# Forget values computed tile by tile, tokens stationary, in the first stage of a hybrid streaming encoder step

## The chip, the cores and the metric

The kernel runs on one core of a Trainium2 chip. The metric is device time in microseconds (us) of one execution; lower is better. The engines are TensorE (PE; its weight loads are a row of their own, PEld), VectorE (DVE), ScalarE (ACT), GpSimd (POOL) and SyncE (SP), which here only issues DMAs. Each engine works through its own instructions in order and waits at semaphores for the others.

## What is computed

One layer of a hybrid encoder, for 1024 tokens of a prompt and 8 x 16 tokens of running streams, 1152 tokens in all, with a model width of 1024:

```python
h = rms_norm(x, ln1)
proj = h @ w_in                       # columns: q 512, k 512, v 512, f 8, xr 512, yg 512
q, k, v, f, xr, yg = jnp.split(proj, SPLITS, axis=-1)
logf = jax.nn.log_sigmoid((f + b_f).astype(jnp.float32))   # one value a token and head
attn = fox_prompt(q, k, v, logf)      # attention with the cumulative sum of logf in its logits
...                                   # conv + RG-LRU on xr, gelu(yg), mixed @ w_out
x = x + jnp.square(jax.nn.relu(h2 @ w_up)) @ w_down
```

The change is about `f`: the product of h (1152 x 1024) with eight columns of `w_in`, the forget values before their log sigmoid.

## The kernel before, in words

All wide products are split: an operand is held as a rounded high part and a remainder (`h_hi`, `h_lo`; `wf_hi`, `wf_lo`; both of type fp32r), and `split_product` issues three matmuls for each of the 8 slices of the contraction (`KC` = 8): high x high, high x low and low x high, on lines 1383, 1384 and 1385, so 24 for one result. Each matmul has its own weight load of its stationary operand (the profile counts 7539 of either); two neighbouring matmuls that share one load it twice. Rows of the profile name the moving operand first and the stationary one second, `psum<-wp_hi,h_hi`.

**First stage.** For each of 9 tiles of 128 tokens (`NT` = 9): SP loads `x_in` into one of three slots, once `turn` of the tile three before has ended (line 405); ACT takes the sum of squares (line 696, one record for the activation and one for reading the accumulator); DVE makes the mean (955), POOL the root (606), DVE normalizes in place (`x_norm`, 959); PE transposes the tile in eight 128x128 pieces into two of four PSUM banks (`turn`, 1399); ACT casts the result to `h_hi` (`turn_hi`, 688) and DVE subtracts to get `h_lo` (`turn_lo`, 966). ACT and DVE do the casts of tile t-2 after the squares or the mean of tile t. `turn(t)` also waits for `h_lo` of tile t-2, whose banks it reuses. After tile 3, PE transposes the small parameter rows (1408). DVE copies them out ahead of `turn_lo(3)` (977).

After the nine tiles ACT and DVE split the forget weights `wf_raw` (704, 985) and then the weights of the first head pair (708, 989). PE computes the forget values: the eight weight columns stationary, 384 tokens moving, three groups (`G` = 3) of 24 matmuls into banks 5 to 7. ACT copies the 8 x 384 results to `f_rows` (715), and PE turns them in nine transposes into 128 tokens x 72 values in bank 4 (1421). DVE adds the bias and starts the log sigmoid (1003 to 1018); PE waits for `l_abs`, which line 1007 signals, because bank 4 is needed next.

**Pair stage.** `pair_pe(0)` projects tile after tile: `project(t)` is 24 matmuls of 384 columns with `h_hi` or `h_lo` of the tile stationary. After `project(1)` PE waits for the normed queries and keys of tile 0 (`turn_qk(0)`, 1456), which need a root from POOL (662). POOL does these roots only after it has built all constants (600 to 651), and it starts on most constants after the root of tile 8. `turn_forgets` follows `project(2)`. Then come the attention of four head pairs, the recurrent part, the output projection and the MLP, in program order throughout. No scheduler reorders anything: the order on each engine is the order written.

Of the kernel before, what the change touches and what calls it, by code (L numbers as in the profile page):

```python
# [7 lines left out]
F32 = mybir.dt.float32  # L8
F32R = mybir.dt.float32r
BF16 = mybir.dt.bfloat16  # L10
ALU = mybir.AluOpType
# [3 lines left out]
P = 128  # L15
# [5 lines left out]
H = 8  # L21
# [6 lines left out]
T_ALL = SEQ + DEC_B * DEC_T  # L28
NT = T_ALL // P
KC = D // P  # L30
G = 3
GN = T_ALL // G
# [27 lines left out]
def streaming_step(nc, x_prompt, x_sample, cache_k, cache_v, cache_logf, state_h, state_conv, ln1, w_in, b_f,  # L60
# [6 lines left out]
    def sem(name):  # L67
        return ctx.enter_context(nc.semaphore(name))

    def sb(scope, name, shape, dt=F32):  # L70
        return scope.enter_context(nc.sbuf_tensor(name, shape, dt))

    h_hi = sb(ctx, "h_hi", [P, KC, T_ALL], F32R)
    h_lo = sb(ctx, "h_lo", [P, KC, T_ALL], F32R)
# [7 lines left out]
    over = ExitStack()  # L82
# [6 lines left out]
    cc = sb(over, "cc", [64, KEYS])  # L89
    c_mid = sb(over, "c_mid", [64, KEYS], BF16)  # L90
    over_pad = sb(over, "over_pad", [P, 64])
    f_rows = sb(over, "f_rows", [H, T_ALL])
    over.close()
    under.close()
    mix = sb(ctx, "mix", [P, KC, T_ALL])
# [1 line left out]
    ident = sb(ctx, "ident", [P, P])  # L97
# [46 lines left out]
    wf_raw = sb(cross, "wf_raw", [P, KC, H])  # L144
    wf_hi = sb(cross, "wf_hi", [P, KC, H], F32R)
    wf_lo = sb(cross, "wf_lo", [P, KC, H], F32R)
# [60 lines left out]
    psum = ctx.enter_context(nc.psum_tensor("psum", [P, 8, 512], F32))  # L207
# [8 lines left out]
    wf_in = sem("wf_in")  # L216
# [8 lines left out]
    h_lo_ready = sem("h_lo_ready")  # L225
    rows_turned = sem("rows_turned")
    wf_split = sem("wf_split")
    f_done = sem("f_done")
    f_copied = sem("f_copied")
    f_turned = sem("f_turned")  # L230
    wf_ready = sem("wf_ready")
    params_copied = sem("params_copied")
    l_abs = sem("l_abs")
# [77 lines left out]
    def two_banks(b):  # L311
        return psum[:, b:b + 2, :].rearrange("p a n -> p (a n)")
# [29 lines left out]
    def step_queries(s):  # L342

        _, qc, kt = attention_step(s)
        return max(kt * P, qc * SPAN), (qc + 1) * SPAN
# [21 lines left out]
    with nc.allow_non_contiguous_dma(reason="narrow columns of small arrays"), nc.Block() as block:  # L367
# [313 lines left out]
        def _(act):  # L681
# [9 lines left out]
            for t in range(NT):  # L691
                act.wait_ge(x_landed[t % 3], 16 * (t // 3 + 1))
                if t >= 1:
                    act.wait_ge(x_squared, t)

                nc.scalar.activation(two_banks(6), x_in[:, t % 3, :], ACT.Square,
                                     accum_out=x_ss[:, t:t + 1]).then_inc(x_squared, 1)
                if t >= 2:
                    turn_hi(t - 2)
            turn_hi(NT - 2)  # L700
            turn_hi(NT - 1)

            act.wait_ge(wf_in, 16)
            nc.scalar.copy(wf_hi[:], wf_raw[:]).then_inc(wf_split, 1)

            def pair_hi(p, j):
                act.wait_ge(raw_in[j], 32 * p + 32)
# [2 lines left out]

            for j in range(4):
                pair_hi(0, j)
            for g in range(G):
                act.wait_ge(f_done, g + 1)
                nc.scalar.copy(f_rows[:, g * GN:(g + 1) * GN], psum[0:H, 5 + g, 0:GN]).then_inc(f_copied, 1)
            act.wait_ge(l_abs, 1)
            nc.scalar.activation(l_e[:], l_e[:], ACT.Exp, scale=-1.0).then_inc(l_exp, 1)

# [228 lines left out]
        def _(dve):  # L947
# [23 lines left out]
            for t in range(NT):  # L971
                x_mean_of(t)
                if t == 5:
                    dve.wait_ge(small_in, 16 * SMALL)
                    nc.vector.tensor_scalar(qgain[:], qgain[:], DH ** -0.5, None, ALU.mult)
                    dve.wait_ge(rows_turned, 1)
                    nc.vector.tensor_copy(param[:, :, 0:ROWS], psum[:, 4, 0:LC * ROWS].rearrange(
                        "p (c r) -> p c r", c=LC)).then_inc(params_copied, 1)
                if t >= 2:
                    turn_lo(t - 2)  # L980
                x_norm(t)
            turn_lo(NT - 2)
            turn_lo(NT - 1)
            dve.wait_ge(wf_split, 1)
            nc.vector.tensor_tensor(wf_lo[:], wf_raw[:], wf_hi[:].bitcast(F32), ALU.subtract).then_inc(wf_ready, 1)

            def pair_lo(p, j):
                dve.wait_ge(w_hi, 4 * p + j + 1)
# [10 lines left out]
            for j in range(4):  # L999
                pair_lo(0, j)  # L1000

            dve.wait_ge(f_turned, 1)
            d.did(nc.vector.tensor_tensor(l_in[:, 0:NT * H].rearrange("p (t h) -> p t h", h=H),
                                          psum[:, 4, 256:256 + NT * H].rearrange("p (t h) -> p t h", h=H),
                                          bf_b[:, None, :].to_broadcast([P, NT, H]), ALU.add))
            d.link(nc.vector.tensor_copy(l_in[:, NT * H:NL], param[:, :, R_LAM]))
            nc.vector.scalar_tensor_tensor(l_e[:], l_in[:], -1.0, l_in[:], ALU.mult, ALU.max).then_inc(l_abs, 1)  # L1007
# [276 lines left out]
            for t in range(NT):  # L1284
# [12 lines left out]
                for half in range(2):  # L1297
                    dve.wait_ge(out_done, 2 * t + half + 1)
                    at = mix[:, 4 * half:4 * half + 4, tile(t)]
                    if half == 0:  # L1300
# [4 lines left out]
                    last = nc.vector.scalar_tensor_tensor(  # L1305
                        at, psum[:, 2 * half + 1, :].rearrange("p (k n) -> p k n", n=P), rs2[:, t % 2, 1:2], at,
                        ALU.mult, ALU.add)
# [72 lines left out]
        def _(pe):  # L1380
            def split_product(out, hi, lo, r_hi, r_lo, n, first=True, end=True):
                for k in range(n):
                    nc.tensor.matmul(out, hi(k), r_hi(k), start=first and k == 0, stop=False)  # L1383
                    nc.tensor.matmul(out, hi(k), r_lo(k), start=False, stop=False)  # L1384
                    last = nc.tensor.matmul(out, lo(k), r_hi(k), start=False, stop=end and k == n - 1)  # L1385
                return last

            def tile(t):
                return slice(t * P, (t + 1) * P)
# [3 lines left out]
            def turn(t):  # L1393
# [3 lines left out]
                for b in range(2):  # L1397
# [2 lines left out]
                                                   x_in[:, t % 3, (4 * b + k) * P:(4 * b + k + 1) * P], ident[:])  # L1400
                    last.then_inc(x_turned, 1)

            for t in range(NT):
                turn(t)
                if t == 3:
                    pe.wait_ge(small_in, 16 * SMALL)
                    for c in range(LC):
                        last = nc.tensor.transpose(psum[:, 4, c * ROWS:(c + 1) * ROWS], rows[:, c * P:(c + 1) * P],
                                                   ident[0:ROWS, 0:ROWS])
                    last.then_inc(rows_turned, 1)  # L1410

            pe.wait_ge(wf_ready, 1)
            pe.wait_ge(h_lo_ready, 2 * NT)
            for g in range(G):
                n = slice(g * GN, (g + 1) * GN)
                split_product(psum[0:H, 5 + g, 0:GN], lambda k: wf_hi[:, k, :], lambda k: wf_lo[:, k, :],
                              lambda k: h_hi[:, k, n], lambda k: h_lo[:, k, n], KC).then_inc(f_done, 1)
            pe.wait_ge(f_copied, G)
            pe.wait_ge(params_copied, 1)
            for t in range(NT):  # L1420
                last = nc.tensor.transpose(psum[:, 4, 256 + t * H:256 + (t + 1) * H], f_rows[:, t * P:(t + 1) * P],
                                           ident[0:H, 0:H])
            last.then_inc(f_turned, 1)
            pe.wait_ge(l_abs, 1)

            def turn_forgets():
# [242 lines left out]
            for c in range(LC):  # L1669
                last = nc.tensor.transpose(psum[0:36, 7, c * P:(c + 1) * P], h_keep[:, c, :], ident[:])  # L1670
# [3 lines left out]
            for t in range(NT):  # L1674
                pe.wait_ge(mix_lo, t + 1)
                for half in range(2):
                    if t >= 1:
                        pe.wait_ge(x1_ready, 2 * t - 1 + half)
                    for part in range(2):
                        if t == 0 and half == 0:  # L1680
                            pe.wait_ge(w_lo, V_OUT + 4 * part + 4)
                        n = slice(half * SPAN, (half + 1) * SPAN)
                        last = split_product(psum[:, 2 * half + part, :],
                                             lambda k: h_hi[:, 4 * part + k, tile(t)], lambda k: h_lo[:, 4 * part + k, tile(t)],
                                             lambda k: wo_hi[:, 4 * part + k, n], lambda k: wo_lo[:, 4 * part + k, n], 4)
# [67 lines left out]
```

## Time and profile before

| | us |
|---|---|
| three runs | 1619.63, 1625.93, 1626.43 |
| median | 1625.93 |
| the profiled execution | 1623.88 |
| its span | 1622.2 |
| PE busy in the span | 1505.5 (93%) |
| first stage: its first to its last transpose on PE | 8.8 to 36.6 |
| forget values on PE | 38.1 to 54.1 |
| first projection of pair 0 starts | 54.8 |

The span reaches from the first to the last recorded instruction; 1.7 us of the profiled execution lie outside it. A row of the timeline gives start, duration, engine, line, operation, moving operand and stationary operand, the shape of the stationary operand (rows*columns) and the number merged; brackets hold the idle time before it and what ended it. Matmuls overlap, so the distance from start to start is the cost of one in a row, and not the duration of its record.

### The profile page before, as it was taken

How to read it: one execution, taken by the hardware profiler on the slowest of the kernel's cores; microseconds unless marked ns; L12 is line 12 of the kernel's file. 1: busy time of each engine (PE TensorE's matmuls, PEld its weight loads, DVE VectorE, ACT ScalarE, POOL GpSimd, SP SyncE). 2: the span in 40 equal slices, each digit the busy share in tenths (PEclk: the TensorE clock that was granted, in tenths of full speed). 3: DMA queues.
4: the chain of work that ended last, by engine and by line, in shares of the span. 5: the costliest groups of instructions: out<-in, count | busy, mean ns of one | idle time of the engine just before them, and what ended most of it. 6: DMA issues, size and time to landing. Idle time of an engine off the chain costs nothing.

```text
span 1622.2 us, 19284 instructions
## 1 busy us (share of the span) xinstructions
PE 1505.5 (93%) x7539; PEld 1290.1 (80%) x7539; DVE 738.9 (46%) x1186; ACT 422.4 (26%) x741; POOL 83.3 (5%) x119
## 2 busy tenths in 40 slices
PE   5979999989989989579989999999999999999997
PEld 3755875875965878568889999889998899998896
DVE  6354154254153154577544444444445444444444
ACT  5114124124123056443232221112221112211110
POOL 3410010010100000010000000000000000000000
PEclk7979799899899889889999999999999999999998
DMA  6023241241331211041111111101111011111004
GB/s 176 8 69 93 76 102 42 71 103 40 86 75 45 59 31 55 28 131 39 40 52 53 53 39 51 37 28 52 52 39 39 26 52 52 46 45 39 26 27 117
DMA packets 133129, 92.87 MB, mean 57 GB/s; under 512 B 22358, under 2 KB 122710, under 8 KB 133076
## 3 DMA queue, kind: packets, MB, share of 16 engines
q1 hardware_dynamic: 133076, 92.14, 19.8%
q8 instruction: 36, 0.59, 0.2%
q14 instruction: 17, 0.14, 0.0%
HBM read 78.24 MB, written 9.68 MB: 54 GB/s over the span
## 4 chain that ended last, share of the span: by engine, by line
PE 86%; DVE 6%; DMA 3%; ACT 2%; issue 1%; SPq 1%; POOL 1%; ACTq 0%; DVEq 0%
PE psum L1383 23%; PE psum L1384 23%; PE psum L1385 23%; PE psum L1521 4%; PE psum L1622 3%; PE psum L1593 1%; PE psum L1505 1%; PE psum L1477 1%; DVE tops L1106 1%; DMA k_c<-in_cache_k_dram 1%; PE psum L1508 1%; PE psum L1643 1%; PE psum L1575 1%; POOL rs L662 1%; DMA v_c<-in_cache_v_dram 1%
## 5 line engine op out<-in xcount | busy, mean ns | idle before, releaser
L1351 DVE TENSOR_TENSOR mix<-psum,mix 128x512 f32<-128x512 f32 x288 | 196.4, 690 | 162.9 <-PE psum L1385 162.9
L1383 PE MATMUL psum<-h_hi,wu_hi 128*128 128x384 f32 x768 | 259.1, 337 | 4.2 <-DVE mix L1305 4.2
L1384 PE MATMUL psum<-h_lo,wu_hi 128*128 128x384 f32 x768 | 258.7, 337 | 0.0
L1385 PE MATMUL psum<-h_hi,wu_lo 128*128 128x384 f32 x768 | 258.6, 337 | 0.0
L1383 PE MATMUL psum<-wd_hi,u_hi 128*128 128x512 f32 x576 | 225.2, 391 | 3.6 <-issue 3.6
L1385 PE MATMUL psum<-wd_hi,u_lo 128*128 128x512 f32 x576 | 225.0, 391 | 0.0
L1384 PE MATMUL psum<-wd_lo,u_hi 128*128 128x512 f32 x576 | 225.0, 391 | 0.0
L1383 PEld LDWEIGHTS psum<-h_hi,wu_hi 128*128 128x128 f32 x768 | 144.9, 189 | 4.9 <-issue 4.4
L1384 PEld LDWEIGHTS psum<-h_lo,wu_hi 128*128 128x128 f32 x768 | 145.0, 189 | 0.5
L1385 PEld LDWEIGHTS psum<-h_hi,wu_lo 128*128 128x128 f32 x768 | 144.9, 189 | 0.0
L922 ACT CAST wd_hi<-raw 128x1024 fp32r<-128x1024 f32 x32 | 32.1, 1049 | 401.4 <-PE psum L1385 399.9
L1383 PEld LDWEIGHTS psum<-wd_hi,u_hi 128*128 128x128 f32 x576 | 108.8, 189 | 26.0 <-issue 4.0
L1385 PEld LDWEIGHTS psum<-wd_hi,u_lo 128*128 128x128 f32 x576 | 108.7, 189 | 22.7
L1384 PEld LDWEIGHTS psum<-wd_lo,u_hi 128*128 128x128 f32 x576 | 108.7, 189 | 22.1
L1343 DVE CAST u_hi<-up 128x384 fp32r<-128x384 f32 x96 | 34.5, 360 | 200.8 <-ACT up L918 200.8
L1383 PE MATMUL psum<-wp_hi,h_hi 128*128 128x384 f32 x288 | 103.0, 357 | 0.7 <-DVE l_e L1007 0.7
L1384 PE MATMUL psum<-wp_lo,h_hi 128*128 128x384 f32 x288 | 99.9, 347 | 0.0
L916 ACT ACTIVATE up<-psum 128x384 f32<-128x384 f32 x96 | 47.0, 490 | 203.0 <-PE psum L1385 203.0
L1385 PE MATMUL psum<-wp_hi,h_lo 128*128 128x384 f32 x288 | 99.7, 346 | 0.0
L1521 PE MATMUL psum<-pt,v 128*128 128x512 f32 (+1 forms) x192 | 85.2, 530 | 2.3 <-ACT pt L762 1.9
L1337 DVE TENSOR_TENSOR wd_lo<-raw,wd_hi 128x1024 fp32r<-128x1024 f32 x32 | 37.9, 1222 | 68.7 <-ACT wd_hi L922 68.7
L1383 PE MATMUL psum<-h_hi,wl_hi 128*128 128x384 f32 x192 | 66.6, 347 | 2.5 <-ACT ti L844 2.0
(253 smaller groups left out, 2254.1 us busy)
## 6 DMA issues: line engine op xcount, KB each, us to landing
raw<-in_w_up_dram SPq DMA_DIRECT2D x32, 512.0 KB, 4.7
raw<-in_w_down_dram SPq DMA_DIRECT2D x32, 512.0 KB, 3.3
v_c<-in_cache_v_dram SPq DMA_DIRECT2D x32, 256.0 KB, 3.5
k_c<-in_cache_k_dram SPq DMA_DIRECT2D x32, 256.0 KB, 3.0
raw<-in_w_in_dram SPq DMA_DIRECT2D x32, 192.0 KB, 3.9
out_dram<-mix SPq DMA_DIRECT2D x9, 512.0 KB
x_in<-in_x_prompt_dram SPq DMA_DIRECT2D x8, 512.0 KB, 4.0
raw<-in_w_in_dram SPq DMA_DIRECT2D x8, 512.0 KB, 5.2
```

Source lines behind the costliest of these rows:

```text
L662: nc.gpsimd.tensor_tensor(rs4[:, t % 2, :], m4[:, t % 2, :], neg_half[:], ALU.pow).then_inc(rs4_ready, 1)
L916: nc.scalar.activation(up[:, m % 3, :], psum[:, up_bank(par, m), 0:GN], ACT.Relu).then_inc(up_read, 1)
L922: nc.scalar.copy(wd_hi[:, k, :], raw[:, k, :]).then_inc(w_hi, 1)
L1106: nc.vector.reduce_max(tops[:, hp, t:t + 1], src, AX_X).then_inc(bound_read, 1)
L1337: nc.vector.tensor_tensor(wd_lo[:, k, :], raw[:, k, :], wd_hi[:, k, :].bitcast(F32), ALU.subtract).then_inc(w_lo, 1)
L1343: d.link(nc.vector.tensor_copy(u_hi[at], up[:, m % 3, :]))
L1351: nc.vector.tensor_tensor(at, psum[:, 4 + 2 * (t % 2) + half, :].rearrange("p (k n) -> p k n", n=P), at, ALU.add).then_inc(y_added, 1)
L1383: nc.tensor.matmul(out, hi(k), r_hi(k), start=first and k == 0, stop=False)
L1384: nc.tensor.matmul(out, hi(k), r_lo(k), start=False, stop=False)
L1385: last = nc.tensor.matmul(out, lo(k), r_hi(k), start=False, stop=end and k == n - 1)
L1521: nc.tensor.matmul(psum[:, (4 if qc == 0 else 0) + hp, a0 - qc * SPAN:SPAN], v1[:, kt, V_COLS[hp]], pt[:, s % 3, 0:a1 - a0], start=kt == 0 ...
L1622: last = nc.tensor.matmul(psum[:, g, b * 32:(b + 1) * 32], v_c[:, b, kt, :], pts[:, 2 * g, kt * P + b * 32:kt * P + (b + 1) * 32], start=F ...
```

## The change

The three wide groups, their copies to `f_rows` and the nine small transposes go. A new function `forgets(t)` computes the forget values of one tile of tokens in 24 matmuls: `h_hi` or `h_lo` of the tile (128x128) is stationary, and the eight columns of `wf_hi` or `wf_lo` move. The result is already 128 tokens x 8 and goes to columns 8t to 8t+7 of bank 5. It stands in PE's program behind `turn(t + 2)`, and the last two stand behind `turn(8)`. For this the split of the forget weights moves to the front: on ACT behind the squares of tile 1, on DVE ahead of `turn_lo(0)`. The sum with the bias now reads bank 5 and waits for `f_done` of all nine tiles.

```diff
@@ ScalarE, first stage
+                if t == 1:
+                    act.wait_ge(wf_in, 16)
+                    nc.scalar.copy(wf_hi[:], wf_raw[:]).then_inc(wf_split, 1)
                 if t >= 2:
                     turn_hi(t - 2)
             turn_hi(NT - 2)
             turn_hi(NT - 1)
-            act.wait_ge(wf_in, 16)
-            nc.scalar.copy(wf_hi[:], wf_raw[:]).then_inc(wf_split, 1)
...
-            for g in range(G):
-                act.wait_ge(f_done, g + 1)
-                nc.scalar.copy(f_rows[:, g * GN:(g + 1) * GN], psum[0:H, 5 + g, 0:GN]).then_inc(f_copied, 1)
@@ VectorE
+                if t == 2:
+                    dve.wait_ge(wf_split, 1)
+                    nc.vector.tensor_tensor(wf_lo[:], wf_raw[:], wf_hi[:].bitcast(F32), ALU.subtract).then_inc(wf_ready, 1)
                 if t >= 2:
                     turn_lo(t - 2)
...
-            dve.wait_ge(wf_split, 1)
-            nc.vector.tensor_tensor(wf_lo[:], wf_raw[:], wf_hi[:].bitcast(F32), ALU.subtract).then_inc(wf_ready, 1)
...
-            dve.wait_ge(f_turned, 1)
+            dve.wait_ge(f_done, NT)
-                                          psum[:, 4, 256:256 + NT * H].rearrange("p (t h) -> p t h", h=H),
+                                          psum[:, 5, 0:NT * H].rearrange("p (t h) -> p t h", h=H),
@@ TensorE
+            def forgets(t):
+
+                pe.wait_ge(h_lo_ready, 2 * t + 2)
+                split_product(psum[:, 5, t * H:(t + 1) * H], lambda k: h_hi[:, k, tile(t)], lambda k: h_lo[:, k, tile(t)],
+                              lambda k: wf_hi[:, k, :], lambda k: wf_lo[:, k, :], KC).then_inc(f_done, 1)
+
             for t in range(NT):
                 turn(t)
...
-            pe.wait_ge(wf_ready, 1)
-            pe.wait_ge(h_lo_ready, 2 * NT)
-            for g in range(G):
-                n = slice(g * GN, (g + 1) * GN)
-                split_product(psum[0:H, 5 + g, 0:GN], lambda k: wf_hi[:, k, :], lambda k: wf_lo[:, k, :],
-                              lambda k: h_hi[:, k, n], lambda k: h_lo[:, k, n], KC).then_inc(f_done, 1)
-            pe.wait_ge(f_copied, G)
+                if t == 2:
+                    pe.wait_ge(wf_ready, 1)
+                if t >= 2:
+                    forgets(t - 2)
+            forgets(NT - 2)
+            forgets(NT - 1)
             pe.wait_ge(params_copied, 1)
-            for t in range(NT):
-                last = nc.tensor.transpose(psum[:, 4, 256 + t * H:256 + (t + 1) * H], f_rows[:, t * P:(t + 1) * P],
-                                           ident[0:H, 0:H])
-            last.then_inc(f_turned, 1)
```

How the order moves on PE in the middle of the first stage. Before, from the transposes of tile 3 to those of tile 4 (shapes in these rows are output rows x columns):

```order
L1399 MATMUL psum<-ident,x_in 128x128 [waits h_lo_ready,x_normed]
L1399 MATMUL psum<-ident,x_in 128x128 x7
L1408 MATMUL psum<-ident,rows 128x42 [waits small_in]
L1408 MATMUL psum<-ident,rows 128x42 x3
L1399 MATMUL psum<-ident,x_in 128x128 [waits h_lo_ready,x_normed]
```

The same place in the changed kernel, from the last matmul of `forgets(0)` on:

```order
L1380 MATMUL psum<-wf_hi,h_lo 128x8
L1394 MATMUL psum<-ident,x_in 128x128 [waits h_lo_ready,x_normed]
L1394 MATMUL psum<-ident,x_in 128x128 x7
L1409 MATMUL psum<-ident,rows 128x42 [waits small_in]
L1409 MATMUL psum<-ident,rows 128x42 x3
L1378 MATMUL psum<-wf_hi,h_hi 128x8 [waits h_lo_ready]
L1379 MATMUL psum<-wf_lo,h_hi 128x8
```

Between two tiles' transposes there now stand 24 matmuls with eight moving columns each.

On PE at the seam to the pair stage, before:

```order
L1384 MATMUL psum<-h_lo,wf_hi 8x384
L1385 MATMUL psum<-h_hi,wf_lo 8x384
L1421 MATMUL psum<-ident,f_rows 128x8 [waits params_copied,f_copied]
L1421 MATMUL psum<-ident,f_rows 128x8 x8
L1383 MATMUL psum<-wp_hi,h_hi 128x384 [waits w_lo,l_abs]
```

The chain of copy and transposes is gone from this place; the projection still waits for `l_abs`, and the groups of 384 columns ahead of it are gone too.

On ACT at the start, before (`psum` here is scrap space for the squares):

```order
L696 ACTIVATE psum,x_ss<-x_in 128x1024 [waits x_landed0]
L696 ACTIVATE psum,x_ss<-x_in 128x1024 [waits x_squared,x_landed1]
L696 ACTIVATE psum,x_ss<-x_in 128x1024 [waits x_squared,x_landed2]
L688 CAST h_hi<-psum 128x4x128 [waits x_turned] x2
L696 ACTIVATE psum,x_ss<-x_in 128x1024 [waits x_squared,x_landed0]
```

and in the changed kernel:

```order
L693 ACTIVATE psum,x_ss<-x_in 128x1024 [waits x_landed0]
L693 ACTIVATE psum,x_ss<-x_in 128x1024 [waits x_squared,x_landed1]
L697 CAST wf_hi<-wf_raw 128x64 [waits wf_in]
L693 ACTIVATE psum,x_ss<-x_in 128x1024 [waits x_squared,x_landed2]
L685 CAST h_hi<-psum 128x4x128 [waits x_turned] x2
```

The squares of tile 2 now stand behind a wait for the forget weights' DMA.

## Rows read from the trace of the kernel before

**Rows 1.** Timeline of PE, 8 to 65 us: the first stage and the seam.
```profile
13.60 1.87 PE L1399 MATMUL psum<-ident,x_in 128*128 128x128 f32 x8 [0.49 <-DVE x_in L959]
19.50 1.97 PE L1399 MATMUL psum<-ident,x_in 128*128 128x128 f32 x8 [4.04 <-DVE x_in L959]
21.41 0.65 PE L1408 MATMUL psum<-ident,rows 42*128 42x42 f32 x4
21.99 1.97 PE L1399 MATMUL psum<-ident,x_in 128*128 128x128 f32 x8
...
34.63 1.97 PE L1399 MATMUL psum<-ident,x_in 128*128 128x128 f32 x8 [1.19 <-DVE x_in L959]
38.13 0.49 PE L1383 MATMUL psum<-h_hi,wf_hi 128*8 128x384 f32 x1 [1.53 <-DVE wf_lo L985]
...
53.37 0.72 PE L1421 MATMUL psum<-ident,f_rows 8*128 8x8 f32 x9 [0.56 <-ACT f_rows L715]
54.77 0.44 PE L1383 MATMUL psum<-wp_hi,h_hi 128*128 128x384 f32 x1 [0.67 <-DVE l_e L1007]
...
64.78 0.27 PE L1456 MATMUL psum<-ident,qk 128*128 128x128 f32 x1
```

**Rows 2.** Weight loads, grouped by line and shape: stationary shape, count, busy us, mean ns.
```profile
L1383 PEld LDWEIGHTS psum<-wp_hi,h_hi 128*128 128x128 f32 x288 | 57.1, 198 | 0.9 <-DVE l_e L1007 0.8 <-issue 0.2
L1384 PEld LDWEIGHTS psum<-wp_lo,h_hi 128*128 128x128 f32 x288 | 56.6, 196 | 0.0
```

**Rows 3.** Timeline of PE: 128x128 stationary, 32 or 1 moving columns; a projection.
```profile
404.93 1.87 PE L1622 MATMUL psum<-pts,v_c 128*128 128x32 f32 x16
411.99 7.03 PE L1622 MATMUL psum<-pts,v_c 128*128 128x32 f32 x32 [1.23 <-DMA v_c<-in_cache_v_dram]
418.83 0.67 PE L1383 MATMUL psum<-wp_hi,h_hi 128*128 128x384 f32 x1
...
691.37 1.01 PE L1656 MATMUL psum<-ones_col,ssq 128*128 128x1 f32 x4 [4.43 <-DVE ssq L1263]
713.63 0.50 PE L1656 MATMUL psum<-ones_col,ssq 128*128 128x1 f32 x4
```

**Rows 4.** Stretches of PE: from:to, length, busy us (instructions), granted clock, DMA share, GB/s.
```profile
20.00:22.00 2.00, 2.00 (x12) 0.50 0.00 0
...
42.00:44.00 2.00, 2.00 (x12) 0.86 0.00 0
...
418.00:419.00 1.00, 1.00 (x6) 0.50 0.00 0
421.00:422.00 1.00, 1.00 (x6) 0.79 1.12 335
```

**Rows 5.** The tile `wf_raw`: DMA and cast, duration ns, start us; time to landing.
```profile
L392 SPq DMA_DIRECT2D wf_raw<-in_w_in_dram x1: 587/587/587, 7.7 to 7.7; - x1
L704 ACT CAST wf_hi<-wf_raw x1: 248/248/248, 37.1 to 37.1; 128x64 fp32r<-128x64 f32 x1
...
DMA to landing us min/median/max: 3.7/3.7/3.7
```

**Rows 6.** Timeline of ACT around tile 2.
```profile
9.35 1.03 ACT L696 ACTIVATE psum<-x_in 128x1024 f32<-128x1024 f32 x1 [0.39 <-DMA x_in<-in_x_prompt_dram]
```

**Rows 7.** Timeline of DVE, the normalizing of tile 2.
```profile
12.26 1.28 DVE L959 SCALAR_TENSOR_TENSOR x_in<-x_in,x_rs,ln_b 128x1024 f32<-128x1024 f32 x1
```

**Rows 8.** Timeline of POOL: last root of the first stage, last constant, first root of pair 0.
```profile
31.86 0.54 POOL L606 TENSOR_TENSOR x_rs<-x_ms,neg_half 128x1 f32<-128x1 f32 x1 [2.32 <-DVE x_ms L955]
...
57.49 0.29 POOL L651 CAST smask<-build 128x128 bf16<-128x128 f32 x1
62.26 1.03 POOL L662 TENSOR_TENSOR rs<-m,neg_half 128x4 f32<-128x4 f32 x1 [4.47 <-DVE m L1076]
```

**Rows 9.** The chain that ended last, pieces of the first stage: start, us, what.
```profile
26.87 3.55 DMA x_in<-in_x_sample_dram
```

**Rows 10.** Line 1622, its weight loads: duration ns min/median/max, first and last start.
```profile
L1622 PEld LDWEIGHTS psum<-pts,v_c x256: 190/333/337, 169.7 to 534.5; 128*128 128x128 f32 x128
```

More of the change, by code:

```diff
@@ L91, in streaming_step @@
     over_pad = sb(over, "over_pad", [P, 64])
-    f_rows = sb(over, "f_rows", [H, T_ALL])
     over.close()
@@ L228, in streaming_step @@
     f_done = sem("f_done")
-    f_copied = sem("f_copied")
-    f_turned = sem("f_turned")
     wf_ready = sem("wf_ready")
```

## The prediction

> **What bounds the kernel now.** I read the page first for what is busy (PE, 93%), then the timeline of PE over the first 65 us, since all edits lie there, then the same stretch of ACT, DVE and POOL for who releases PE. Up to 36.6 us PE is not the bound: each tile's transposes take 1.97 us, and PE waits between tiles for the normed tile [rows 1]. From 38.13 us, when the last `h_lo` and `wf_lo` are there, PE alone sets the pace: 72 matmuls for the forget values, then copy and transposes, 0.67 us for DVE, and the projection at 54.77 us [rows 1]. So 16.6 us lie between the last tile and the pair stage, and the question is whether the new work fits into PE's gaps before.
>
> The stretches show one thing more: in the first stage PE runs at a granted clock of 0.50, its 1.2 GHz level, even where it is busy for 2.00 of 2.00 us with transposes [rows 4]. The forget stream of 384 moving columns started at that level too and rose to the full level (2.4 GHz) between 42 and 44 us [rows 4].
>
> **What is removed.** 38.13 to 54.77 us on PE: 16.64 us [rows 1], with three copies on ACT and the transposes.
>
> **What one `forgets` costs.** It is 24 matmuls with 24 loads of a 128x128 stationary operand; before, the stationary operand had only 8 columns [rows 1]. The kernel before has two groups that hold such a stationary operand against few moving columns, and both show that the load sets the distance. With 32 moving columns, 16 take 1.87 us at the full level: (1.87 - 0.20)/15 = 0.111 us each, where 0.20 is about one record; 32 take 7.03 us at half: (7.03 - 0.40)/31 = 0.214 us [rows 3]. With one moving column, four take 0.50 and 1.01 us, again about 0.11 and 0.21 us each [rows 3]. So eight columns cost the same: one `forgets` is 24 x 0.214 = 5.13 us at half level, or 24 x 0.111 = 2.7 us at the full one. These rows are f32 and the new ones fp32r; I take them as equal, since the loads of fp32r `h_hi` last 198 ns in the mean, most at the full level [rows 2], against 190 ns for the shortest f32 ones [rows 10].
>
> **Which level.** The change rests on this. The 32 matmuls at 411.99 us keep PE busy without a gap for 7 us, with the same loads, and the clock stays at 0.50 to their end; it rises only at 421 to 422 us, when PE has been at the 384-column projection for over 2 us [rows 3, 4]. Transposes don't raise it either [rows 4]. The streak at 404.93 us was at the full level, but it came out of work that had it [rows 3]. The new stage is transposes and load-bound matmuls alone and begins at half level. I take 0.50 throughout. The Trainium skill ("TensorE: Matmul & The Clock Gate", "Why this matters for your kernels") says that a TensorE kept busy continuously gets to the full clock; by that rule the new stage, which has no gap, would run at the full level, which is the first rival below. The stream at 411.99 us speaks against it.
>
> **The moved split.** The DMA of `wf_raw` is issued at 7.66 us and lands 3.7 us later, at 11.4 us [rows 5]. ACT, which took the squares of tile 2 at 9.35 us [rows 6] and then the casts of tile 0, now waits until 11.4, casts the weights (0.25 us [rows 5]) and starts those squares at 11.6. Queued behind it: the casts of tile 0, for them `turn_lo(0)` on DVE, and behind that `x_norm(2)`, now at 12.26 us [rows 7]. By the old distances ACT is through with the squares at 12.8, `h_hi(0)` stands at 13.35 and 13.85, `x_norm(2)` starts at 14.6, and `turn(2)` at 15.9 us instead of 13.60 [rows 1]. This slip of 2.3 us vanishes for later tiles if PE has room (tile 3 is released at 19.5 by its own DMA), but here it starts PE's queue.
>
> **The sum at half level.** PE from 15.9 us on, without a gap, at 1.91 us for eight transposes (19.50 to 21.41) and 0.58 us for the parameter rows (21.41 to 21.99) [rows 1]: 7 turns x 1.91 = 13.4, parameters 0.6, 9 x 5.13 = 46.2, together 60.2, so the last matmul issues by 76.1 and ends at 76.3 us. Does PE ever wait in it? `turn(3)` could start at 19.50 and comes at 22.9; each later turn comes 7.0 us after the one before, against about 3.2 us now ((34.63 - 21.99)/4 [rows 1]), so normed tiles and DMAs are always ahead; also tile 6, whose load may start at 24.8 (end of `turn(3)`) and takes 3.6 us [rows 9] while its turn is due at 44.6. `forgets(7)` and `forgets(8)` follow the last turn (60.6) by 5 and 10 us and find `h_lo` ready. Weights of the first pair are split by ACT and DVE from 61 to 67 us, beside PE. Then 0.68 us for DVE as before: the projection starts at 76.9 us instead of 54.77, **22.1 us later**.
>
> Behind that nothing changes in order, so I carry the shift to the end. POOL has its constants done 25.4 us after the root of tile 8 (from 32.4, the root's end, to 57.78: 25.4) [rows 8]; that root comes at about 45 us, the constants end near 71, before the first root of the pair stage is wanted (84). The projection begins at half level, as the one at 418.83 us did, which rose some 2.5 us later [rows 3, 4]; half level for 2.5 us costs at most 1.3 us, which I leave out of the sum and in the range. The profiled execution took 1623.88 us, which is also the mean of the three runs (1624.0) and 2.05 us below their median. 1623.9 + 22.1 = 1646.0.
>
> **Rivals.**
>
> *The clock rises in the stage.* If PE reaches the full level at 22 us, after the first `forgets`, a tile costs 1.04 + 2.7 = 3.7 us and the sum gives: `turn(3)` 22.5, `turn(8)` 41.3 to 42.4, `forgets(8)` to 50.5, projection at 51.3, 3.5 us earlier. But then POOL is next: the load of tile 8 starts after `turn(5)` (31.2) and takes 3.6 us, so its root comes near 36.3 instead of 31.86, constants end at 62.2, the root of the first pair tile at 63.2 and `turn_qk(0)` at 64.3, against 64.78 now [rows 1, 8, 9]. About 0.5 us gained: 1623.4, no slowdown. It decides if the granted clock is above 0.9 over the stage. If it is high in parts only, each microsecond at the full level saves one, and the time lies between: 1630 to 1642. For it: PE would be busy 100%. Against it: rows 3 and 4 as read above.
>
> *The load is cheaper.* If a load of fp32r hid half of itself, or the second load of the same `h_hi` cost little, 24 would take about 3.4 us (a third of the loads gone) at half level: a tile 5.3 us, 60.2 - 9 x 1.7 = 44.9, projection at 61.6, 6.8 us later, 1630.7. Against it: the loads of the wide projection, where the same pair of neighbours occurs, are all counted and equally long, line 1384 repeating the load of 1383 [rows 2]. The Trainium skill (same page, "LDWEIGHTS") gives P/1.2 ns, 107 ns for 128 columns; rows 3 agree at the full level and show double at half. By the page's 107 ns a `forgets` would be 2.6 us at either level, a tile 4.5 us, and the projection would come near 54 us: about 1623.
>
> *The load is dearer.* If load and matmul don't overlap with another type or with alternating `h_hi` and `h_lo`, the distance could reach the duration of one record, 0.40 us: 9 x 24 x 0.19 = 40 us more, 1687. The neighbours with few columns exclude most of this.
>
> *The change is worth what it says:* with the new work wholly in the gaps, about 15 us less, 1609. For this PE would need 2.7 us of gap for each tile at full level and POOL's constants out of the way; rows 1 show gaps of 0.5 to 4 us and rows 8 a floor at 57.8.
>
> **How the numbers follow.** Half level with 0.21 us: 0.77, 1643 to 1652 with the run-to-run spread. Full level: 0.07. High in parts: 0.06. Cheaper loads: 0.06. Dearer: 0.03. Full gain: 0.01. The predicted time is 1646. Eight in ten need the first case and the upper part of the mixed ones: 1637 to 1652. A measurement of this kernel tells 0.5% (8 us) from no change. Faster by over 0.5%: 0.02; within: 0.14; slower: 0.84.
>
> **What would show it.** The first stage of the profile after: `forgets` as 24 matmuls in about 5.1 us at a clock of 0.50; PE without gaps from `turn(2)`, at 15.9, to 76 us; turns 7.0 us apart; 216 loads of 128x128 with a mean of about 333 ns, as most of line 1622 [rows 10]; the squares of tile 2 at 11.6; projection at 76.9. A clock of 1.00 in the stage, or distances under 0.15 us at 0.50, would make the prediction wrong, and so would a pair stage that takes back some of the shift.

## The result, and the profile after

The changed kernel takes 1647.36 us (median of four runs, 1646.36 to 1648.38), the kernel before 1624.46 us (four runs, 1619.63 to 1626.43): a ratio of 1.0145, 95% interval 1.0121 to 1.0170, or 22.9 us more. The forecast was 1646.0 us.

The timeline of PE in the first stage after the change, which answers to [rows 1] (start us, duration, engine, line, operation, operands, shape of the stationary operand, shape of the moving one):

```profile
15.50 1.97 PE L1394 MATMUL psum<-ident,x_in 128*128 128x128 f32 x8 [2.34 <-DVE x_in L953]
17.12 0.36 PE L1378 MATMUL psum<-wf_hi,h_hi 128*128 128x8 f32 x1
17.33 0.35 PE L1379 MATMUL psum<-wf_lo,h_hi 128*128 128x8 f32 x1
17.55 0.35 PE L1380 MATMUL psum<-wf_hi,h_lo 128*128 128x8 f32 x1
...
22.24 1.97 PE L1394 MATMUL psum<-ident,x_in 128*128 128x128 f32 x8
24.14 0.65 PE L1409 MATMUL psum<-ident,rows 42*128 42x42 f32 x4
...
29.86 1.97 PE L1394 MATMUL psum<-ident,x_in 128*128 128x128 f32 x8
36.60 1.97 PE L1394 MATMUL psum<-ident,x_in 128*128 128x128 f32 x8
...
73.59 0.35 PE L1380 MATMUL psum<-wf_hi,h_lo 128*128 128x8 f32 x1
74.66 0.66 PE L1378 MATMUL psum<-wp_hi,h_hi 128*128 128x384 f32 x1 [0.72 <-issue]
...
77.04 0.52 PE L1379 MATMUL psum<-wp_lo,h_hi 128*128 128x384 f32 x1
77.36 0.52 PE L1380 MATMUL psum<-wp_hi,h_lo 128*128 128x384 f32 x1
...
79.27 0.34 PE L1378 MATMUL psum<-wp_hi,h_hi 128*128 128x384 f32 x1
79.45 0.34 PE L1379 MATMUL psum<-wp_lo,h_hi 128*128 128x384 f32 x1
...
85.10 0.27 PE L1451 MATMUL psum<-ident,qk 128*128 128x128 f32 x1
```

The new matmuls start 0.213 us apart though only eight columns move, 24 of them take 5.12 us (17.12 to 22.24), and from the transposes of tile 2 on PE has no gap: the brackets with idle time are gone until 74.66 us. Tiles follow 6.74 us apart instead of 3.2, and the projection starts 19.9 us later than in [rows 1]. The weight loads by line, which answer to [rows 2] (count, busy us, mean ns):

```profile
L1380 PEld LDWEIGHTS psum<-wf_hi,h_lo 128*128 128x128 f32 x72 | 24.0, 333 | 0.0
L1379 PEld LDWEIGHTS psum<-wf_lo,h_hi 128*128 128x128 f32 x72 | 24.0, 333 | 0.0
L1378 PEld LDWEIGHTS psum<-wf_hi,h_hi 128*128 128x128 f32 x72 | 24.0, 333 | 0.1
```

All but one of the 216 last 332 to 337 ns (the one 287), the long duration that line 1622 has at the lower clock [rows 10]. The column of the granted clock needs care here. PE by stretches, to be read beside [rows 4] (from:to, length, busy us, instructions, granted clock, DMA share, GB/s):

```profile
16.00:20.00 4.00, 4.00 (x21) 1.00 0.40 139
68.00:72.00 4.00, 4.00 (x20) 1.00 0.01 2
76.00:78.00 2.00, 2.00 (x7) 1.00 0.00 0
79.00:80.00 1.00, 1.00 (x8) 1.00 0.08 4
```

It reads 1.00 throughout, but between 78 and 79 us the 384-column matmuls of the projection go from 0.32 to 0.18 us apart, as they do where the column shows a step from 0.50 to 1.00. The durations are of the lower level until then. The column shows 1.00 although PE runs at half pace, up to the first change of the clock that the trace has; the trace of the kernel before does the same for its first transposes (1.94 us for eight at 8.76 us).

### The profile page after: what moved, and what is told of

Its sections match the earlier page's. It is cut to its first block, busy times and chain, and to the rows that moved or that the text cites. A ratio compares the mean times of both kernels' runs of the same rounds, so it can differ in the third digit from the quotient of the medians.

```text
span 1645.8 us, 19550 instructions
## 1 busy us (share of the span) xinstructions
PE 1536.5 (93%) x7674; PEld 1333.3 (81%) x7674; DVE 742.0 (45%) x1186; ACT 421.6 (26%) x738; POOL 85.8 (5%) x119
## 4 chain that ended last, share of the span: by engine, by line
PE 87%; DVE 6%; DMA 2%; ACT 2%; issue 1%; POOL 1%; SPq 1%; ACTq 0%; DVEq 0%
PE psum L1378 24%; PE psum L1379 23%; PE psum L1380 23%; PE psum L1516 4%; PE psum L1617 3%; PE psum L1588 2%; PE psum L1500 1%; PE psum L1472 1%; DVE tops L1101 1%; PE psum L1503 1%; PE psum L1638 1%; PE psum L1570 1%; DMA k_c<-in_cache_k_dram 1%; PE psum L1394 1%; POOL rs L659 1%
```

## The experiments

The theory: what the change costs is 216 loads of a 128x128 stationary operand, each 0.213 us at the lower clock whatever moves, and nothing in the changed stage raises the clock. The rivals: the earlier split of the weights, the place between the tiles, and a cost that goes with moving columns.

**The split alone** (`e1_split_only`): the kernel before with this; the same lines behind the loop go (not shown).

```diff
@@ ScalarE
+                if t == 1:
+                    act.wait_ge(wf_in, 16)
+                    nc.scalar.copy(wf_hi[:], wf_raw[:]).then_inc(wf_split, 1)
@@ VectorE
+                if t == 2:
+                    dve.wait_ge(wf_split, 1)
+                    nc.vector.tensor_tensor(wf_lo[:], wf_raw[:], wf_hi[:].bitcast(F32), ALU.subtract).then_inc(wf_ready, 1)
```

> The kernel before with only the split of the forget weights moved to the front, on ScalarE behind the squares of tile 1 and on VectorE ahead of the remainder of tile 0. My theory (the load-bound matmuls make the whole loss): the transposes of tile 2 start about 2 us later (15.5 instead of 13.6), tile 3 is released at 19.5 by its own DMA as before, the projection starts within 0.5 us of 54.8, time 1624 within 4 us. The rival (the wait for the weights' DMA on ScalarE delays the whole chain of tiles): projection about 2 us later and about 1627.

Measured: 1624.68 us against 1624.41, ratio 0.9998 (0.9986 to 1.0010). The timeline of PE:

```profile
15.55 1.82 PE L1399 MATMUL psum<-ident,x_in 128*128 128x128 f32 x8 [2.77 <-DVE x_in L959]
19.39 1.97 PE L1399 MATMUL psum<-ident,x_in 128*128 128x128 f32 x8 [2.02 <-DVE x_in L959]
...
34.72 1.10 PE L1399 MATMUL psum<-ident,x_in 128*128 128x128 f32 x8 [1.59 <-DVE x_in L959]
...
54.74 0.44 PE L1383 MATMUL psum<-wp_hi,h_hi 128*128 128x384 f32 x1 [0.79 <-DVE l_e L1007]
...
63.17 0.27 PE L1456 MATMUL psum<-ident,qk 128*128 128x128 f32 x1
```

Tile 2 slips by 2.0 us, tile 3 by nothing, and the projection stands where it was. The split costs nothing by itself. The last row is of use below: with the same code from 54.7 us on, this execution turns the first queries at 63.17 us, the one of [rows 1] at 64.78. From 56 to 60 us the granted clock is 1.00 here and 0.57 there. So 1.6 us there is the state of the clock in one execution.

The row at 34.72 us shows something that [rows 4] don't: eight transposes in 1.10 us instead of 1.97. PE had done nothing but transposes with gaps (busy 1.51 of 2.00 us from 30 to 32 us), and yet the clock went up:

```profile
30.00:32.00 2.00, 1.51 (x7) 0.50 1.17 325
34.00:36.00 2.00, 1.10 (x8) 1.00 0.64 150
```

**The same matmuls behind the last tile** (`e2_forgets_last`).

```diff
-                if t == 2:
-                    pe.wait_ge(wf_ready, 1)
-                if t >= 2:
-                    forgets(t - 2)
-            forgets(NT - 2)
-            forgets(NT - 1)
+            pe.wait_ge(wf_ready, 1)
+            for t in range(NT):
+                forgets(t)
```

> The changed kernel with all nine groups of 24 matmuls behind the last tile instead of between the tiles. My theory (216 weight loads at 0.213 us, clock at its lower level): from about 38 us on 46 us of PE, projection at about 84.8, time 8 to 11 us above the changed kernel, 1656 to 1659. The rival (transposes in between hold the clock down, a pure stream of these matmuls would raise it): after some 4 us the distance falls to 0.11 us, projection at about 65, time about 1636. A second rival (the placement between the tiles is what costs): no slower than the changed kernel.

Measured: 1653.01 us, ratio 1.0171 (1.0153 to 1.0188), 28.6 us above before and 5.7 above the changed kernel, less than the 8 to 11 expected. The timeline of PE:

```profile
36.26 0.35 PE L1378 MATMUL psum<-wf_hi,h_hi 128*128 128x8 f32 x1
36.47 0.35 PE L1379 MATMUL psum<-wf_lo,h_hi 128*128 128x8 f32 x1
...
81.06 0.35 PE L1378 MATMUL psum<-wf_hi,h_hi 128*128 128x8 f32 x1
...
83.20 0.66 PE L1378 MATMUL psum<-wp_hi,h_hi 128*128 128x384 f32 x1 [0.72 <-issue]
```

46 us of these matmuls in a row, without a gap or a transpose, keep 0.213 us from first to last. So transposes don't hold the clock down; this stream does not raise it either. The place between the tiles is better than the place behind them. The stream starts at 36.3 and not at 38, since the first group waits only for early tiles: of the miss, this is 1.6 us. The projection starts 8.5 us later than in the changed kernel and the span is 7.7 us longer; why the medians differ by 5.7 only, no run shows.

**256 moving columns** (`e3_256_moving`): the eight weight columns repeated 32 times.

```diff
-                split_product(psum[:, 5, t * H:(t + 1) * H], lambda k: h_hi[:, k, tile(t)], lambda k: h_lo[:, k, tile(t)],
-                              lambda k: wf_hi[:, k, :], lambda k: wf_lo[:, k, :], KC).then_inc(f_done, 1)
+                split_product(psum[:, 5, t * H:t * H + 256].rearrange("p (a h) -> p a h", h=H),
+                              lambda k: h_hi[:, k, tile(t)], lambda k: h_lo[:, k, tile(t)],
+                              lambda k: wf_hi[:, k, None, :].to_broadcast([P, 32, H]),
+                              lambda k: wf_lo[:, k, None, :].to_broadcast([P, 32, H]), KC).then_inc(f_done, 1)
```

> The changed kernel with the eight weight columns repeated 32 times as moving operand, 256 columns for each matmul; the result of a tile is in the first eight, the rest is overwritten by the next tile. My theory (the load alone sets the distance, and the clock stays low because so few columns move): in the first few us still 0.21 us a matmul although 32 times as many columns move, then the clock rises and the distance falls to about 0.11 us; projection at 49 to 53 us, and the end held by POOL's constants: 1621 to 1626. The rival (the clock has nothing to do with it, and columns come on top of the loads): 0.21 us plus 0.21 us each, projection at about 120 us, 1690. In between (load and matmul overlap but the clock stays): 1647 as the changed kernel.

Measured: 1626.39 us, ratio 1.0017 (1.0006 to 1.0027), 0.4 above the expected range. With 32 times the columns the stage is faster. The timeline of PE, and then PE by stretches with the granted clock (which in this execution changed before the stream began, so that the column agrees with the distances):

```profile
17.55 0.42 PE L1379 MATMUL psum<-wf_lo,h_hi 128*128 128x256 f32 x1
17.76 0.42 PE L1380 MATMUL psum<-wf_hi,h_lo 128*128 128x256 f32 x1
...
20.95 1.04 PE L1394 MATMUL psum<-ident,x_in 128*128 128x128 f32 x8
25.07 1.04 PE L1394 MATMUL psum<-ident,x_in 128*128 128x128 f32 x8
...
49.57 0.41 PE L1378 MATMUL psum<-wp_hi,h_hi 128*128 128x384 f32 x1 [1.21 <-issue]
...
62.65 0.48 PE L1453 MATMUL psum<-ident,qk 128*128 128x128 f32 x1 [4.51 <-DVE qk L1084]
```

```profile
16.00:18.00 2.00, 2.00 (x12) 0.50 0.14 55
18.00:20.00 2.00, 2.00 (x14) 0.68 0.68 221
20.00:22.00 2.00, 2.00 (x19) 1.00 0.10 41
```

At 0.50 the distance is 0.21 us as with eight columns, so 248 columns more cost nothing beside the load. Then the clock rises to 1.00 and stays until PE waits at 58 us; the distance falls to 0.112 us, transposes take 1.04 us instead of 1.97, the projection starts at 49.57 us, 25.1 us before that of the changed kernel. It was the lower clock that made 216 loads cost 46 us; at 0.112 us each they are 24 us. But of those 25.1 us only 22.4 are left at 62.65 us, where PE waits 4.5 us for the normed queries, and DVE for a root from POOL. POOL's timeline shows its constants ending just before:

```profile
60.41 0.29 POOL L648 CAST smask<-build 128x128 bf16<-128x128 f32 x1
```

**Fewer loads** (`e4_joined`): high and low weight columns side by side, 16 moving columns.

```diff
+                for k in range(KC):
+                    nc.tensor.matmul(psum[:, 5, t * 2 * H:(t + 1) * 2 * H], h_hi[:, k, tile(t)], wf_both[:, k, :],
+                                     start=k == 0, stop=False)
+                    last = nc.tensor.matmul(psum[:, 5, t * 2 * H:(t + 1) * 2 * H], h_lo[:, k, tile(t)], wf_both[:, k, :],
+                                            start=False, stop=k == KC - 1)
```

> The changed kernel with high and low weight columns side by side as one moving operand of 16 columns, so that each high or low part of a tile is loaded once: 16 matmuls a tile instead of 24, and one more VectorE addition at the end (the product low x low comes along). My theory (cost = number of loads of 128x128): 16 x 0.213 = 3.4 us a tile, 72 loads less are 15.4 us, the projection at about 59.6, time 1632 to 1633. The rival (cost goes with moving columns): 16 columns take as long as two of 8, saving nothing to 5 us, 1642 to 1647.

Measured: 1631.45 us, ratio 1.0035 (1.0021 to 1.0049), 15.9 us below the changed kernel and just below the 1632 to 1633 expected. The timeline of PE, and one stretch of it (this trace too has a change of the clock ahead of the stream):

```profile
31.22 1.97 PE L1395 MATMUL psum<-ident,x_in 128*128 128x128 f32 x8
...
36.26 1.97 PE L1395 MATMUL psum<-ident,x_in 128*128 128x128 f32 x8
...
59.32 0.66 PE L1379 MATMUL psum<-wp_hi,h_hi 128*128 128x384 f32 x1 [0.99 <-issue]
```

```profile
20.00:40.00 20.00, 20.00 (x96) 0.50 0.48 139
```

A tile is 5.04 us against 6.74: eight loads less at 0.213 are 1.70. Twice the columns cost nothing, and the granted clock stands at 0.50. With this the size of the term is shown from both sides, by number and by clock.

In all these kernels there are as many matmuls as loads, so their number doesn't tell the price of a load from a fixed price of a matmul. A group of [rows 1] does: the nine transposes of `f_rows`, whose loads are 8 rows high, take 0.72 us at the full level, (0.72 - 0.20)/8 = 0.065 us each, where matmuls with an f32 load of 128x128 are 0.111 us apart. So a matmul with a small load is cheaper, and what is above that goes with the large load; this is shown at the full level only.

**The wide form, moved into the loop** (`e5_wide_in_loop`).

```diff
+                if t in (4, 7):
+                    forget_group((t - 4) // 3)
+            forget_group(2)
...
+                split_product(psum[0:H, (5, 5, 6)[g], 0:GN], lambda k: wf_hi[:, k, :], lambda k: wf_lo[:, k, :],
+                              lambda k: h_hi[:, k, n], lambda k: h_lo[:, k, n], KC).then_inc(f_done, 1)
```

> The kernel before (eight weight columns stationary, 384 tokens moving) with the split moved to the front as in the changed kernel and the three wide groups moved up: groups 0 and 1 behind the transposes of tiles 4 and 7, group 2 behind the last tile. My theory: 24 matmuls of 384 columns are 4.2 to 7.7 us for three tiles, against 15.4 for three groups of the changed form, so they fit into the gaps; projection at 44 to 48 us. Then POOL is late: it ends its constants at about 58 us, the first queries and keys are turned at about 60.5 instead of 64.8, and of 8 us some 4 arrive at the end: about 1620. The rival (POOL does not hold the pair stage): 1614 to 1617.

Measured: 1622.05 us, ratio 1.0000 (0.9986 to 1.0013). The timeline of PE:

```profile
45.13 0.45 PE L1388 MATMUL psum<-wp_hi,h_hi 128*128 128x384 f32 x1 [0.67 <-DVE l_e L1012]
...
61.21 0.47 PE L1467 MATMUL psum<-ident,qk 128*128 128x128 f32 x1 [5.91 <-DVE qk L1094]
```

The projection gains 9.6 us, and PE gives 5.9 of them back waiting. By the time nothing can be told from no change; the mechanism was as expected, its gain smaller.

**POOL's constants between the roots.** Two kernels (`e6_wide_pool_early` on the one before, `e7_256_pool_early` on the one with 256 columns) test that wait; POOL's instructions are the same, in another order and with one more wait behind each root. The order, the pieces being functions that hold the old lines:

```diff
+            root(0)
+            small_parts()
+            root(1)
+            n.link(nc.gpsimd.memset(v1[:, :, DH:P], 1.0))
+            root(2)
+            operands(0, 0)
+            root(3)
+            operands(0, 1)
+            root(4)
+            small_masks()
...
+            root(8)
+            rows_select(1)
```

> The kernel of the wide groups in the loop (label e5_wide_in_loop), and on POOL the constants built in pieces between the roots of the first stage instead of behind the last root. My theory (in that kernel POOL is what is late): the constants end before 50 us, projection at 45 to 49 us, the first queries and keys turned at 54 to 58, time 3 to 6 us below that kernel, about 1616. The rival (POOL was not it, or the pieces delay the roots and with them the tiles): no gain, or a slower first stage, 1620 or more.

> The kernel with 256 moving columns (label e3_256_moving), and on POOL the constants in pieces between the roots. There PE waited 4.5 us for POOL's root before the first queries and keys were turned (62.65 us). My theory: without it they are turned at about 58 to 59 us, time 4 us below that kernel, about 1622. The rival: the wait moves to another engine and nothing arrives, 1626.

Measured: 1615.70 us, ratio 0.9955 (0.9938 to 0.9972), and 1617.95 us, ratio 0.9974 (0.9961 to 0.9987): 6.4 and 8.4 us below the kernels with late constants, the first a little more than expected, the second twice as much. Projection and first queries of the kernel with 256 columns:

```profile
50.14 0.42 PE L1400 MATMUL psum<-wp_hi,h_hi 128*128 128x384 f32 x1 [0.72 <-issue]
...
58.55 0.27 PE L1475 MATMUL psum<-ident,qk 128*128 128x128 f32 x1
```

The wait is gone, which is 4.1 us (62.65 to 58.55). Behind the wait PE's matmuls run at the lower clock in `e3_256_moving` (granted clock 0.50 from 62 to 66 us and 0.73 from 66 to 68) and at 1.00 here; some 4.4 us at half pace are about 2.2 us by estimate. Where the other 2 us of the medians come from no run settles; the spans of the two profiled executions differ by 5.8 us, not by 8.4.

**All together** (`e8_joined_256_pool_early`): 16 loads a tile, 256 columns, constants early; and the same without early constants (`e10_joined_256`).

```diff
+                    out = psum[:, 5, t * 2 * H:t * 2 * H + 256].rearrange("p (a h) -> p a h", h=2 * H)
+                    w = wf_both[:, k, None, :].to_broadcast([P, 16, 2 * H])
+                    nc.tensor.matmul(out, h_hi[:, k, tile(t)], w, start=k == 0, stop=False)
+                    last = nc.tensor.matmul(out, h_lo[:, k, tile(t)], w, start=False, stop=k == KC - 1)
```

> Token-stationary form with all that the runs so far suggest: high and low weight columns side by side (16 loads a tile instead of 24), repeated 16 times to 256 moving columns, POOL's constants in pieces between the roots. My theory: 16 x 0.111 = 1.8 us a tile at the full clock and 1.05 us of transposes are less than the 3.2 us at which tiles arrive, so the chain of loads, norms and transposes sets the stage again: projection at 41 to 44 us, time 1611 to 1616. The rival (in the gaps the clock falls back, the matmuls cost 3.4 us a tile): projection at 50 to 58 us, 1620 to 1628.

> The joined form with 256 moving columns (label e8_joined_256_pool_early), with POOL's constants left where they were. My theory: projection at about 45 us, PE then waits some 6 to 8 us for the first root, the first queries and keys are turned at 61 to 62 us instead of 54, time 7 us above that kernel, about 1621. The rival (POOL's order matters little): within 2 us of 1614.

Measured: 1614.31 us, ratio 0.9953 (0.9937 to 0.9969), within the 1611 to 1616 expected though its projection starts at 45.55 and not at 41 to 44 us, the fastest kernel here, though `e6_wide_pool_early` is not to be told from it; and 1622.01 us, ratio 0.9990 (0.9979 to 1.0000), 7 to 8 us more for the late constants. The timeline of PE in the first, then in the second:

```profile
37.53 1.09 PE L1417 MATMUL psum<-ident,x_in 128*128 128x128 f32 x8 [0.50 <-DVE x_in L975]
...
45.55 0.41 PE L1401 MATMUL psum<-wp_hi,h_hi 128*128 128x384 f32 x1 [1.08 <-DVE l_e L1025]
...
53.95 0.27 PE L1478 MATMUL psum<-ident,qk 128*128 128x128 f32 x1
```

```profile
44.18 0.41 PE L1379 MATMUL psum<-wp_hi,h_hi 128*128 128x384 f32 x1 [1.17 <-issue]
...
61.13 0.47 PE L1456 MATMUL psum<-ident,qk 128*128 128x128 f32 x1 [8.39 <-DVE qk L1085]
```

Now PE waits for tiles again (0.50 us), as it did before the change, and the projection starts 9 us ahead of [rows 1]. Without early constants it starts even 1.4 us earlier, and PE waits 8.4 us.

**Early constants alone** (`e9_before_pool_early`): the kernel before with POOL's order changed.

> The kernel before with nothing changed but POOL's constants in pieces between the roots. My theory (POOL is late only once PE reaches the pair stage before about 50 us): there the first root of the pair stage waits for VectorE, not for POOL's constants, so projection at 54 to 56 us and time within 3 us of before. The rival (the constants beside PE's and VectorE's work cost something by themselves, so that part of the gain of the kernels with early constants has nothing to do with the forget values): 1617 to 1620.

Measured: 1625.48 us, ratio 1.0006 (0.9991 to 1.0020). POOL's constants end at 46 us there, and nobody had waited for them. The roots come 1 us later, and so does the projection (56.00 us). So the gain of the kernels with early constants is not a gain of its own: POOL's order is worth nothing until PE is early.

What each kernel does to the first turned queries, against the medians (before is the median of the same comparison, 1624.41, 1623.21 or 1623.55 us; the changed kernel's 1624.46):

| kernel | projection starts | first queries turned | median | less before |
|---|---|---|---|---|
| before | 54.77 | 64.78 | 1624.46 | |
| changed | 74.66 | 85.10 | 1647.36 | +22.9 |
| `e1_split_only` | 54.74 | 63.17 | 1624.68 | +0.3 |
| `e2_forgets_last` | 83.20 | 93.07 | 1653.01 | +28.6 |
| `e3_256_moving` | 49.57 | 62.65 | 1626.39 | +2.0 |
| `e4_joined` | 59.32 | 69.68 | 1631.45 | +7.0 |
| `e5_wide_in_loop` | 45.13 | 61.21 | 1622.05 | -1.2 |
| `e6_wide_pool_early` | 46.26 | 56.26 | 1615.70 | -7.5 |
| `e7_256_pool_early` | 50.14 | 58.55 | 1617.95 | -5.3 |
| `e8_joined_256_pool_early` | 45.55 | 53.95 | 1614.31 | -8.9 |
| `e9_before_pool_early` | 56.00 | 66.09 | 1625.48 | +1.9 |
| `e10_joined_256` | 44.18 | 61.13 | 1622.01 | -1.5 |

The end follows the column of the first queries better than that of the projection: the median less the first queries is 1559.4 to 1563.7 us over the twelve rows, the median less the projection 1567.8 to 1577.8. The medians and the two columns are of different executions, so a difference of 1 or 2 us between two rows tells nothing.

## Why the prediction was right, step by step

- **The cost of one `forgets`**: 5.13 us forecast, 5.12 measured. That f32 and fp32r loads cost the same, taken from neighbours, holds: 0.213 us with 8 columns, with 16 and at the lower clock with 256. Neither of the rivals about the load came: cheaper ones would have given 3.4 us, dearer ones about 0.40 us each.
- **The level**: the lower one throughout, as the stream at 411.99 us [rows 3] had shown; `e2_forgets_last` shows it for 46 us on end and `e3_256_moving` shows what the other level would have brought. The rule of the Trainium skill ("TensorE: Matmul & The Clock Gate", "Why this matters for your kernels") that a TensorE kept busy continuously reaches the full clock does not hold in this stage: in the busy sense of the profile it is at 4.00 of 4.00 us, and does not rise. One premise was wrong, "Transposes don't raise it either": it came from one stretch of [rows 4], and `e1_split_only` has transposes at a granted clock of 1.00 from 34 to 36 us. In the profiled execution of the changed kernel nothing came of it, for which the forecast had given no ground. My test for it, "a clock of 1.00 in the stage", was a bad one: the column says 1.00 and the durations say otherwise. The other half of the test, distances, was the one to rely on.
- **The moved split**: the weights landed after 3.3 us, not 3.7; the squares of tile 2 started at 11.32 and `turn(2)` at 15.50, forecast 11.6 and 15.9. It costs nothing alone, as said.
- **The sum**: the projection was forecast at 76.9 us and came at 74.66. The term that was mis-sized is the turn, 1.91 us taken from transposes followed by transposes of another shape (19.50 to 21.41). Followed by a matmul of `forgets` it occupies PE for 1.62 us (15.50 to 17.12); seven turns make 6 x 0.29 = 1.7 us, the one ahead of the parameter rows keeping 1.90, and tile 2's start the other 0.4.
- **The carry to the end**: the forecast carried 22.1 us unchanged. Measured, the shift is 19.9 us at the projection, 20.3 at the first queries and 23.6 in the spans (1622.2 to 1645.8). So 2.2 us too many before the projection met 3.7 that arose behind it, and that the total came out closer than its parts is luck. From projection to first queries the changed kernel takes 10.44 us, the one before 10.01 in [rows 1] and 8.43 in `e1_split_only`. The start at the lower level, priced at 1.3 us at most and left out of the sum, cost 2.0 against the latter, and the old execution had 1.6 us of the same. Of the 3.3 us behind the first queries, 2.7 arise in the streams of 32 moving columns, between the two blocks of `pts,v_own`: in the first pair 7.09 us before (169.50 to 176.59) and 8.17 after (189.93 to 198.10), in the second 6.05 (287.83 to 293.88) and 7.72 (308.89 to 316.61); in the third and fourth they agree within 0.01. These streams run at either level, depending on when the clock falls. The same code in `e1_split_only` has 7.93 and 7.43 us there, and from its first queries to the end of its span it takes 1560.6 us, against 1557.4 in the execution before and 1560.7 in the changed one. So an old form can be as slow as the changed one: the 3.3 us belong to the executions, and no run shows them as a cost of the change.
- **Cover that was named**: POOL's constants were no bound here (first root at 82.5 us), and the rival's floor was real: with the clock raised the gain ended at POOL as that rival said, at 62.65 us and not at 64.3, and the time at 1626.4 where it said 1623.4.

The stream behind the first block of the second pair, its second 16 matmuls: before, `e1_split_only` and after.

```profile
290.42 2.27 PE L1622 MATMUL psum<-pts,v_c 128*128 128x32 f32 x16
```

```profile
289.20 3.46 PE L1622 MATMUL psum<-pts,v_c 128*128 128x32 f32 x16
```

```profile
311.95 3.46 PE L1617 MATMUL psum<-pts,v_c 128*128 128x32 f32 x16
```

The same 16 matmuls take 2.27 us in one execution and 3.46 in the two others, one of them of the old form, by the level of the clock.

## What to carry to other kernels

Before operands are exchanged so that fewer columns move, count the loads: one of 128x128 in f32 or fp32r cost 0.11 us at the full clock and 0.21 us at the lower one, and up to 256 moving columns hid behind it. Then ask what the stream does to the clock: here many wasted columns were 21 us faster than few useful ones. And where work leaves the start of a stage, look for the engine that was busy beside it: POOL's constants, free before, took back 6 to 8 us of the medians until they were moved.

## What the runs showed of the hardware

- A stream of matmuls with 8 moving columns and 128x128 loads kept PE busy for 46 us without raising its clock (`e2_forgets_last`), and one with 16 did no better (`e4_joined`, 0.50 from 20 to 40 us). The instructions of the changed kernel with 256 columns had it at 1.00 from 20 us on, having begun at 17.2 at the lower level (`e3_256_moving`).
- Transposes with gaps between the tiles had the clock at 1.00 in one execution (`e1_split_only`, 34 to 36 us) and at 0.50 in another ([rows 4], 20 to 22 us).
- At the lower clock 8, 16 and 256 moving columns all start 0.213 us apart with a 128x128 load of fp32r each; at the full one 256 start 0.112 us apart.
- The granted clock of a stretch reads 1.00 where no change has been recorded yet, even at half pace; the distance of like instructions tells the level.
